# A streaming encoder step on one core: PV products of attention cut in pieces, and another order of query tiles

## The reference

```
logits = einsum('bthd,btkhd->bthk', q, k_sel) * HEAD_DIM ** -0.5
probs  = softmax(where(valid, logits, -inf))
out    = einsum('bthk,btkhd->bthd', probs, v_sel)
```

## Time and profile before

| | |
|---|---|
| median of 3 runs | 1749.43 us (1748.06 to 1749.51) |
| profiled execution | 1749.91 us, span 1747.8 us |
| PE / weight loads / DVE / ACT / POOL busy | 92% / 79% / 51% / 36% / 28% |
| granted clock, whole span | 0.975 |
| attention block | 453.3 to 642.2 us |

### The profile page before, as it was taken

How to read it: one execution, slowest core, us unless ns; L and a number is a source line. 1 busy time by engine, 2 the same in 40 slices (tenths; PEclk the granted TensorE clock), 3 DMA queues, 4 the chain that set the end, 5 groups by cost and what they waited for, 6 DMA issues and landing times. The chain is left out here.

```text
span 1747.8 us, 23114 instructions
## 1 busy us (share of the span) xinstructions
PE 1602.2 (92%) x8523; PEld 1388.6 (79%) x8523; DVE 899.6 (51%) x1381; ACT 630.3 (36%) x1303; POOL 486.8 (28%) x335
## 2 busy tenths in 40 slices
PE   5988999999677779998999999999999999999995
PEld 4975999877455557877878888988888888888884
DVE  6338999896454445422664433334344333343438
ACT  5346577952566643223643111111111111111112
POOL 5133111146655513113023222212111222121216
PEclk9999999999799999999999999999999999999999
DMA  5122211111210015222142111111101111111006
GB/s 198 57 67 61 85 49 37 61 63 40 59 29 23 7 45 173 90 91 80 42 145 85 61 49 48 36 48 36 48 24 48 48 48 37 47 36 48 30 19 180
DMA packets 88198, 108.28 MB, mean 62 GB/s; under 512 B 6080, under 2 KB 65216, under 8 KB 88128
## 3 DMA queue, kind: packets, MB, share of 16 engines
q1 hardware_dynamic: 88128, 107.35, 19.8%
HBM read 88.05 MB, written 19.28 MB: 61 GB/s over the span
## 5 line engine op out<-in xcount | busy, mean ns | idle before, releaser
L155 POOL TENSOR_TENSOR w_lo_ring<-w_raw_ring,w_hi_ring 128x1024 fp32r<-128x1024 f32 (+1 forms) x97 | 237.5, 2460 | 814.0 <-ACT w_hi_ring L149 813.5
L2064 DVE TENSOR_TENSOR f_y<-f_y,ps 128x512 f32<-128x512 f32 (+1 forms) x288 | 195.7, 685 | 257.7 <-PE ps L200 257.7
L186 PE MATMUL ps<-hth,w_hi_ring 128*128 128x384 f32 (+2 forms) x1176 | 267.8, 331 | 4.2 <-PEq L1748 1.8
L186 PE MATMUL ps<-htl,w_hi_ring 128*128 128x384 f32 (+2 forms) x1176 | 266.2, 330 | 0.0
L186 PE MATMUL ps<-hth,w_lo_ring 128*128 128x384 f32 (+2 forms) x1176 | 266.2, 330 | 0.0
L200 PE MATMUL ps<-w_hi_ring,f_fh 128*128 128x512 f32 (+1 forms) x576 | 226.8, 394 | 18.8 <-DVE f_y L2064 18.8
L200 PE MATMUL ps<-w_hi_ring,f_fl 128*128 128x512 f32 (+1 forms) x576 | 224.6, 390 | 0.0
L200 PE MATMUL ps<-w_lo_ring,f_fh 128*128 128x512 f32 (+1 forms) x576 | 224.6, 390 | 0.0
L186 PEld LDWEIGHTS ps<-hth,w_hi_ring 128*128 128x128 f32 (+1 forms) x1176 | 203.5, 189 | 8.2 <-issue 5.3
L186 PEld LDWEIGHTS ps<-htl,w_hi_ring 128*128 128x128 f32 (+1 forms) x1176 | 202.8, 188 | 0.6
L186 PEld LDWEIGHTS ps<-hth,w_lo_ring 128*128 128x128 f32 (+1 forms) x1176 | 202.8, 188 | 0.6
(11 more groups left out here) (243 smaller groups left out, 2574.3 us busy)
## 6 DMA issues: line engine op xcount, KB each, us to landing
w_raw_ring<-in_w SPq DMA_DIRECT2D x64, 512.0 KB, 3.8
w_raw_ring<-in_w_in SPq DMA_DIRECT2D x24, 512.0 KB, 3.8
n_xin<-in_x_prompt SPq DMA_DIRECT2D x8, 512.0 KB, 6.0
w_raw_ring<-in_w_o SPq DMA_DIRECT2D x8, 512.0 KB, 3.8
oe_x<-in_x_prompt SPq DMA_DIRECT2D x8, 512.0 KB, 4.9
x<-oe_new SPq DMA_DIRECT2D x8, 512.0 KB, 5.3
me_x<-x SPq DMA_DIRECT2D x8, 512.0 KB, 4.1
x<-me_new SPq DMA_DIRECT2D x8, 512.0 KB, 5.0
```

Of the source, the lines that this page charges most:

```text
L155: pool.tensor_tensor(self.lo[:, slot, 0:width], self.raw[:, g % 2, 0:width], self.hi[:, slot, 0:width].bitcast(F32), ALU.subtract).then_in ...
L186: last = pe.matmul(c.ps[0:width, bank + b, 0:size], part[:, slot, k * width:(k + 1) * width], x[:, k, o:o + size], start=(k == 0 and n == ...
L2064: dve.tensor_tensor(out, out, ps[0:r, u % 2, :], ALU.add).then_inc(y_added, 1)
```

## The change

The order of tiles becomes 0, 1, 7, 2, 6, 3, 5, 4, sample. The low part's PV (now ready at position 5) is cut in 4 + 2 passes, the high part's (position 7) in 4 + 4 + 6; each piece stands behind the transposes of one step, from the head's own last step to the next head's step 3. The sample product comes one step later. DVE's `leave` follows after 6 steps in place of 5. On POOL the split of w_o moves behind the next pair's operands. Nothing else is changed: the same passes, transposes, copies and loads run.

```diff
--- before.py
+++ after.py
@@ -1133,11 +1133,14 @@
     sm = m.put("h_s", [P, 3, SEQ])
     low = m.put("h_low", [P, 4])
 
-    ORDER = [0, 7, 1, 6, 2, 5, 3, 4, NP]
+    ORDER = [0, 1, 7, 2, 6, 3, 5, 4, NP]
     UNITS = HEADS * NT
-    EVENT = {6: 0, 7: 1, 8: NP // 4}
+    EVENT = {5: 0, 7: 1, 8: NP // 4}
     EVENTS = list(EVENT)
-    LEAVE = {6: 0, 7: 1, 8: 2}
+    LEAVE = {5: 0, 7: 1, 8: 2}
+
+
+    CHUNKS = [(5, 3, 0, 4), (5, 4, 4, 6), (7, 3, 0, 4), (7, 4, 4, 8), (7, 5, 8, 14), (8, 4, 0, 3)]
     PIECES = 5
     assert all(max(ORDER.index(i) for i in range(4 * q, 4 * q + 4)) == x for x, q in EVENT.items() if q < NP // 4)
 
@@ -1284,7 +1287,7 @@
 
                 raw = c.w.raw[:, 1:2, :]
                 pool.wait_ge(wo_in, 16 * (p + 1))
-                stack_lo.wait(pool, p, 6)
+                stack_lo.wait(pool, p + 1 if p < NG - 1 else p, 3 if p < NG - 1 else 6)
                 pool.tensor_copy(c.w.hi[:, p:p + 1, :], raw).then_inc(wo_hi, 1)
                 pool.wait_ge(wo_hi, p + 1)
                 pool.tensor_tensor(c.w.lo[:, p:p + 1, :], raw, c.w.hi[:, p:p + 1, :].bitcast(F32), ALU.subtract).then_inc(wo_lo, 1)
@@ -1292,11 +1295,11 @@
 
             for p in range(1, NG):
                 stacks.make_los(pool, p - 1, 1)
-                split(p - 1)
 
                 pool.wait_ge(qk_done, 2 * NT * (p - 1) + NT)
                 stacks.make_his(pool, p, 0)
                 stacks.make_los(pool, p, 0)
+                split(p - 1)
             stacks.make_los(pool, NG - 1, 1)
             split(NG - 1)
 
@@ -1340,7 +1343,7 @@
                         half, o = slice(64 * a, 64 * a + 64), 512 * part + 256 * a
                         dve.tensor_tensor(c.cat[rows, p, o:o + 256], ps[half, 6 + part, 0:256], rsum[half, 0:256], ALU.mult).then_inc(pv_out, 1)
 
-            for g in range(UNITS + 5):
+            for g in range(UNITS + 6):
                 if g < UNITS:
                     hd, p, hh, i = unit(g)
                     r, n = rows_of(i), len(halves(LIM[i]))
@@ -1355,8 +1358,8 @@
                     copies(g - 2)
                 if 0 <= g - 3 < UNITS and (g - 3) % NT in LEAVE:
                     reciprocals(g - 3)
-                if g >= 5 and (g - 5) % NT in LEAVE:
-                    leave(g - 5)
+                if g >= 6 and (g - 6) % NT in LEAVE:
+                    leave(g - 6)
 
         @block.tensor
         def _(pe):
@@ -1404,50 +1407,52 @@
                         last = pe.transpose(ps[0:k, 4 + q % 2, x * r:(x + 1) * r], sm[0:r, g % 3, j * P:j * P + k], c.ident[0:r, 0:r])
                     last.then_inc(tr_done, 1)
 
-            def output(g):
+            def output(g, first, end):
 
                 hd, p, hh, i = unit(g)
                 x = g % NT
                 rows = slice(64 * hh, 64 * hh + 64)
                 v = vs[:, p % 2, :, rows]
-                pe.wait_ge(act_copied, copies_end(g, "act"))
-                pe.wait_ge(dve_copied, copies_end(g, "dve"))
-                if x == EVENTS[0] and hh == 0:
-                    pe.wait_ge(v_in[p % 2], 16 * V_DMAS * (p // 2 + 1))
                 q = EVENT[x]
+                if first == 0:
+                    pe.wait_ge(act_copied, copies_end(g, "act"))
+                    pe.wait_ge(dve_copied, copies_end(g, "dve"))
+                    if x == EVENTS[0] and hh == 0:
+                        pe.wait_ge(v_in[p % 2], 16 * V_DMAS * (p // 2 + 1))
                 if q == NP // 4:
 
                     pe.wait_ge(pv_out, pieces_end(hd, 0))
                     for j in range(3):
                         k = P if j < 2 else DEC
                         last = pe.matmul(ps[rows, 6, 0:DEC], v[0:k, NP + j, :], pts[0:k, j, :], start=(j == 0), stop=(j == 2))
-                else:
-                    if hd:
-                        pe.wait_ge(pv_out, pieces_end(hd - 1, 2 if q == 0 else 1))
-                    tiles = pt[:].rearrange("p (b n) -> p b n", n=P)
-                    for j in range(4 * q + 4):
-                        for a in range(2):
-                            i0 = 4 * q + 2 * a
-                            if j > i0 + 1:
-                                continue
-                            half = slice(64 * a, 64 * a + 64)
-                            if j <= i0:
-                                at = MOFF[i0] // P + j
-                                moving = tiles[:, at:at + i0 + 2:i0 + 1, :]
-                                out = ps[half, 6 + q, 0:256].rearrange("p (t n) -> p t n", t=2)
-                            else:
-                                moving = tiles[:, MOFF[i0 + 1] // P + j, :]
-                                out = ps[half, 6 + q, P:256]
-                            last = pe.matmul(out, v[:, j, :], moving, start=(j == 0), stop=(j == i0 + 1))
-                last.then_inc(pv_done, 1)
-
-            for g in range(UNITS + 4):
+                    last.then_inc(pv_done, 1)
+                    return
+                if hd and first == 0:
+                    pe.wait_ge(pv_out, pieces_end(hd - 1, 2 if q == 0 else 1))
+                tiles = pt[:].rearrange("p (b n) -> p b n", n=P)
+                passes = [(j, a) for j in range(4 * q + 4) for a in range(2) if j <= 4 * q + 2 * a + 1]
+                for j, a in passes[first:end]:
+                    i0 = 4 * q + 2 * a
+                    half = slice(64 * a, 64 * a + 64)
+                    if j <= i0:
+                        at = MOFF[i0] // P + j
+                        moving = tiles[:, at:at + i0 + 2:i0 + 1, :]
+                        out = ps[half, 6 + q, 0:256].rearrange("p (t n) -> p t n", t=2)
+                    else:
+                        moving = tiles[:, MOFF[i0 + 1] // P + j, :]
+                        out = ps[half, 6 + q, P:256]
+                    last = pe.matmul(out, v[:, j, :], moving, start=(j == 0), stop=(j == i0 + 1))
+                if end == len(passes):
+                    last.then_inc(pv_done, 1)
+
+            for g in range(UNITS + 5):
                 if g < UNITS:
                     logits(g)
                 if 0 <= g - 2 < UNITS:
                     transposes(g - 2)
-                if 0 <= g - 3 < UNITS and (g - 3) % NT in EVENT:
-                    output(g - 3)
+                for x, after, first, end in CHUNKS:
+                    if 0 <= g - after < UNITS and (g - after) % NT == x:
+                        output(g - after, first, end)
                 if g >= 4 and (g - 4) % NT in LEAVE:
                     sums(g - 4)
```

## The result

The changed kernel takes 1735.14 us (median of 4, 1734.82 to 1737.37) against 1749.47 us before (median of 4); the ratio is 0.9923, with a 95% interval of 0.9901 to 0.9946. It is faster by 14.3 us. I had forecast 1716, faster by 34, with a range from 1707 to 1732, so the direction was right and the size was more than double what came. The cause turned out to be one wait that I left out.

A forecast was written before the change was run, and what follows sets the result against it. No engine was full; the attention block's heads were bound by their order of work, with PE idling on waits. Gains by head and tail summed to 33.7 us, from 1749.91 to 1716.2, stated as 1716, range 1707 to 1732.

The forecast's parts named there:

- Length of an odd head: Odd heads: PE's 16.3 us plus 0.5 for borders and 1.3 for DVE copy waits, 18.1 us; gain 4.1.
- the nine steps: An odd head's steps followed with each engine's durations, giving 17.5 us without borders.
- Order: New tile order: copies don't wait; the sample product's 1.6 us wait and PE's later bank wait go.
- Length of an even head: Even heads: ACT's third high copy and POOL's chain behind it decide, 19.0 us; gain 3.8, bounds 18.3 and 21.
- First and second head: First head 17.7 becomes 16.8 us; second, with half its cold-clock cost, 19.7, gain 3.8.
- Last head and tail: Last head to its last logits 16.0 us; from there to the end 9.5 against 14.5, gain 5.0.
- The sum: Gains over all heads and the tail add to 33.7 us, taking 1749.91 to 1716.2; stated as 1716.
- POOL's order: Moving the split of w_o behind the next pair's copies costs nothing; without this cover at most 1 us a pair.
- (a): Even heads stay tied to POOL; only odd heads, the last and the tail gain, 21.4 us: 1728; chance 0.12.
- (b): Pieces delay the next mask and exp; heads 20 to 20.5 us, some 15 to 20 gained: 1732; chance 0.10.
- my own signs: Odd heads above 20 us point to (b), even above 21 to (a), odd-head clock below 0.9 to (c).
- (c): PE's clock stays low from odd starts to head ends; 1767 with three odd heads, 1784 with four; chance 0.04.

The follow-up runs named there:

- after: The changed kernel in its first measurement and profile, against the kernel before: 1735.14 us, ratio 0.9923.
- both: Changed kernel with separate rsum columns for the sample tile's sums and DVE's departures back to five steps: 1716.38 us, ratio 0.9814.
- leave_five: Changed kernel with only DVE's departures moved back from six to five steps behind: 1717.07 us, ratio 0.9828.
- both_hi_early: The kernel of both, with ACT's three high copies one position earlier and a wait for low operands ahead of them: 1714.16 us, ratio 0.9805.
- pool_old: Changed kernel with the split of w_o back ahead of the next pair's operands on POOL: 1733.81 us, ratio 0.9927.
- after_again: The changed kernel run once more as it is: 1734.65 us, ratio 0.9910.
- order_whole: Changed kernel with PV products whole again, three steps behind, and departures at five steps; new tile and POOL orders kept: 1731.44 us, ratio 0.9922.
- before_own: The kernel before, with only separate rsum columns added for the sample tile's sums: 1747.01 us, ratio 0.9978.

## Why the prediction was wrong

*The step that failed* is the list of PE's waits in *Length of an odd head* ("0.5 for borders and 1.3 for what stays of the waits for DVE's copies"), in "PE alone would need some 18.4" for an even head, and in the nine steps that I "followed". None has a term for PE's wait for ACT's `h_rsum`; it was put at nothing without a reason. ACT's copy of the sample sums has a wait in front of it, for the departure of the part before, since all parts share 256 columns of `rsum`. Under the old distances it was met in time: the list of the kernel before has no such wait. The diff's line from five to six steps moves the departure behind tile 6's mask. *Order* looks at that line only for who waits for the low part's departure (the sample product). *Length of an odd head* does name the row on DVE, mask of tile 6, copy, high part's departure, next mask, but takes it as a bound for DVE alone, not as something that holds ACT and through it PE. The wait costs 2.1 us in an odd head and 1.5 in an even one (20.29 - 18.18, 21.06 - 19.57): 4 x 2.1 + 3 x 1.5 = 12.9 us. An even head loses less because POOL's chain would have held it at 19.6 anyway. Falls of the clock, most of them behind it, were worth 2.2 us in the first profile and some 6 in the second (174.8 against 168.4 without any). 12.9 and 2.2 are nearly all of the 15.4 us between after's block (170.6) and that of both (155.2).

*Length of an odd head*: 18.1 forecast, 18.18 measured once the wait is away. The sum holds, but no run prices its terms one by one, and they didn't all come: of 18.2 us PE was busy 17.1 (the sixth head in leave_five), and of the 1.3 us for DVE's copies that head shows 0.9.

*Length of an even head*: 19.0 forecast, 19.57 measured in leave_five, and for the reason given. ACT's third high copy ends 10.4 us into the head in place of 9.8: ACT sees the sums at 2.5 us in place of 2.0, and its work from there to the copy's end takes 7.87 us in place of 7.75. POOL's 8.95 us follow, and both_hi_early shows that this chain is the bound. In the changed kernel itself it is not. There POOL is through at 511.04, and PE begins the odd head only at 513.66, still late from the wait:

```profile
508.53 2.51 POOL L625 TENSOR_TENSOR h_qs<-qt,h_qs 64x1088 fp32r<-64x1088 f32 x1 [0.17 <-issue]
...
513.66 0.33 PE L1377 MATMUL ps<-h_kh,h_qs 128*128 128x128 f32 x1
```

*First and second head*: 16.8 forecast, 16.9 measured by first logits and 16.6 by masks. Of the second I had taken half the cold start's price (19.7); without the wait it was 18.1 with the clock at 1.00 (both) and 19.67 at 0.91 (leave_five); with the wait 20.2 at 1.00 (after) and 23.8 at 0.78 (pool_old).

*Last head and tail*: to the last logits 16.0 forecast, 18.0 measured, the wait's 2.1 in it. From there 9.5 forecast and 10.7 measured (615.4 to 626.1). The wait for `h_rsum` has no part in that: PE's steps took 9.8 us where I had added up 8.6, and the last departure 0.9 as forecast.

*The sum.* Without the wait, both's ratio of 0.9814 gives about 1717, next to my 1716. That is luck in part: even heads and tail were longer than forecast by 1.7 (3 x 0.57) and 1.2 us, and the second head, warm, 1.6 shorter. The lower end of the range, 1707, is 1 to 2 us below what the terms' own bounds give, and the 1725 uses 19 and 20.5 for the heads where the terms had said 19.8 and 21. Neither changes the verdict, since 1735 lies above 1732.

*POOL's order*: cost nothing, as forecast, in both forms.

*The rivals.* (a) would have had even heads near 22.8 at full clock, (b) heads of 20 to 20.5 with the copies' waits in place. The time 1735 is close to (b)'s 1732, but its mechanism isn't it: the pieces land in idle time, and leave_five keeps them all and has 18.2. By my own signs odd heads above 20 us (20.3) pointed to (b) and even heads above 21 (21.06) to (a), and it was neither: the signs couldn't tell this wait from them. (c), the clock: falls were there, though never for a whole head. My reading for it was wrong in one point: before, the clock is back at 1.00 at 521.8 us, ahead of the 14-pass block and not inside it. The rule of the Trainium skill (TensorE: Matmul & The Clock Gate, "A second HAM failure mode: psum-queue depth-cycling") isn't borne out by the steady heads: at 18.2 us a head, with small gaps alone, the clock stays at 1.00. The changed kernel's falls from the third head on stand behind one gap of 2.4 to 2.6 us.

## What to carry to other kernels

When a step is moved in one engine's program, ask for each buffer that it reads or frees who may write it next, and who stands behind that writer in its queue; the wait that matters can be two engines away. A buffer shared by parts that leave at different steps is such a link, and 64 columns more cut it. A schedule followed from a trace's durations can be right to 0.1 us in an odd head and still wrong by half the gain for one semaphore left out, so write down every wait of every instruction before adding up.

## What the runs showed of the hardware

With the same instructions, heads at full clock repeat within 0.03 us, inside an execution and from after to after_again (20.27 to 20.29). What wanders is the clock: in after and after_again a gap of 2.4 to 2.6 us of PE is followed by a stretch of 3 to 4 us at 1.2 GHz in some heads and not in others, at 0.9 to 1.4 us each. Shorter gaps went before a fall too: 1.7 to 1.9 us at each odd start of the kernel before from the fourth head on, 1.5 us in order_whole's fifth head. Outside the block, where all kernels have the same instructions, the profiled executions took from 1553.9 us (before_own) to 1562.1 us (after), so two single profiles compared by their spans can't tell less than 8 us, while head lengths at full clock can tell 0.1.
